# Projections with the tokens as weights: the sample's 32 tokens in full f32 through four column tiles

## The reference, cut to what matters

```python
# layer 0: v is the second half of the projection, then a layer norm over it
uv = jax.nn.gelu(x @ w_in)                 # x: (tokens, 1024), w_in: (1024, 4096)
u, v = uv[..., :D_A], uv[..., D_A:]        # D_A = 2048
# between the layers: keys and values of three branches
kv = (rmsnorm(h, kv_norm) @ kv_w)          # kv_w: (1024, 1536)
# layer 1: queries (and gates)
proj = xn @ w_in                           # the first 1024 columns are the queries
```

## Time and profile before

| | us |
|---|---|
| median of 3 runs (1818.1 to 1823.41) | 1822.81 |
| the profiled execution, its own time | 1806.65 |
| its span, first to last instruction | 1804.4 |

### The profile page before, as it was taken

One profiled execution on the slowest core, in us unless ns is written; L12 is line 12 of the kernel. 1 busy time (PEld: TensorE's weight loads), 2 busy tenths in 40 slices (PEclk: granted clock), 3 DMA queues, 4 the chain that ended last, 5 costly groups with the idle time before them and its releaser, 6 DMA issues.

```text
span 1804.4 us, 32338 instructions
## 1 busy us (share of the span) xinstructions
PE 1702.9 (94%) x13254; PEld 1583.0 (88%) x13254; DVE 804.7 (45%) x1326; ACT 537.7 (30%) x872; POOL 79.4 (4%) x134
## 2 busy tenths in 40 slices
PE   6999999999999999998999776999878999999998
PEld 6998899998999999997999544566568999999998
DVE  4325542344333333356164647986445333333333
ACT  4224211222222112133232434765342222212211
POOL 0000000000000000000000002543000000000000
PEclk8999888998999999998999987999998999999999
DMA  4292121222222222222232341000722222222221
GB/s 146 71 315 70 58 66 47 85 94 71 91 73 93 94 81 82 82 84 69 70 125 54 117 130 52 2 1 27 245 60 92 70 83 81 93 93 92 72 76 67
DMA packets 139296, 156.74 MB, mean 87 GB/s; under 512 B 11730, under 2 KB 127746, under 8 KB 138786
## 3 DMA queue, kind: packets, MB, share of 16 engines
q1 hardware_dynamic: 139122, 155.41, 27.0%
q10 hardware_dynamic: 80, 0.02, 0.0%
HBM read 149.58 MB, written 14.16 MB: 91 GB/s over the span
## 4 chain that ended last, share of the span: by engine, by line
PE 88%; DVE 4%; SPq 3%; issue 2%; ACT 2%; DMA 1%; DVEq 0%; ACTq 0%
PE PS L544 58%; PE PS L570 15%; PE PS L870 2%; PE PS L884 2%; PE PS L897 2%; SPq L486 2%; SPq L488 1%; PE PS L678 1%; PE PS L675 1%; PE PS L984 1%; PE PS L950 1%; PE PS L851 1%; PE PS L620 1%; ACT wh L1078 1%; PE PS L937 0%
## 5 line engine op out<-in xcount | busy, mean ns | idle before, releaser
L1401 DVE TENSOR_TENSOR wl<-raw,wh 128x2048 fp32r<-128x2048 f32 x106 | 242.7, 2290 | 410.5 <-ACT wh L1078 410.5
L544 PE MATMUL PS<-act0h,wh 128*128 128x272 f32 x1792 | 378.3, 293 | 10.7 <-DVE act0l L1874 5.9
L544 PE MATMUL PS<-act0l,wh 128*128 128x272 f32 x1792 | 376.0, 291 | 0.0
L544 PE MATMUL PS<-act0h,wl 128*128 128x272 f32 x1792 | 375.7, 291 | 0.0
L1078 ACT ACTIVATE wh<-raw 128x2048 fp32r<-128x2048 f32 x106 | 202.6, 1911 | 433.6 <-PE PS L544 432.2
L544 PEld LDWEIGHTS PS<-act0h,wh 128*128 128x128 f32 x1792 | 287.0, 192 | 11.6 <-DVE wl L1401 6.1
L544 PEld LDWEIGHTS PS<-act0l,wh 128*128 128x128 f32 x1792 | 286.4, 192 | 0.0
L544 PEld LDWEIGHTS PS<-act0h,wl 128*128 128x128 f32 x1792 | 285.8, 191 | 0.0
L570 PE MATMUL PS<-wh,act0h 128*128 128x256 f32 x560 | 161.0, 288 | 7.5 <-DVE act0l L1488 7.5
L570 PE MATMUL PS<-wl,act0h 128*128 128x256 f32 x560 | 159.4, 285 | 0.0
L570 PE MATMUL PS<-wh,act0l 128*128 128x256 f32 x560 | 159.3, 284 | 0.0
(11 more groups left out here) (270 smaller groups left out, 2327.7 us busy)
## 6 DMA issues: line engine op xcount, KB each, us to landing
raw<-in_ffn_w_gate SPq DMA_DIRECT2D x44, 512.0 KB
raw<-in_ffn_w_up SPq DMA_DIRECT2D x44, 512.0 KB
raw<-in_a_w_in SPq DMA_DIRECT2D x32, 512.0 KB
raw<-in_ffn_w_down SPq DMA_DIRECT2D x32, 512.0 KB
raw<-in_a_w_out SPq DMA_DIRECT2D x16, 512.0 KB
crows<-in_cache_kv_cmp SPq DMA_DIRECT2D x64, 128.0 KB, 2.1
cache<-in_cache_kv_slc SPq DMA_DIRECT2D x32, 256.0 KB, 5.0
cache<-in_state_kv_win SPq DMA_DIRECT2D x8, 1024.0 KB, 7.8
```

The source lines that it names most:

```text
L544: mm = pe.matmul(PS[:, 4 * ps + 2 * mt + h, 0:HALF], W[:, rs, k, mt * P:mt * P + P], Xp[:, k * T + h * HALF:k * T + h * HALF + HALF], star ...
L1401: dve.tensor_tensor(wl[:, rs, :, :], raw[:, rs, :, :], wh[:, rs, :, :].bitcast(F32), ALU.subtract).then_inc(w_ready, 1)
```

## The change

In the eighteen token-weight blocks the fifth token tile goes. In its place the 32 sample tokens are the stationary operand of 8 full f32 matmuls (no split: `few` holds the normed f32 activations, `raw` the f32 weights), each in one of four column tiles of 32: feature tile k goes to PSUM partitions 32 (k % 4) onward of bank 4*ps + 2, feature tiles 4 to 7 being added to 0 to 3. ScalarE copies the resulting 128 x 256 partial sums to SBUF (`part`), and one more full f32 matmul with a 128 x 32 selector (`sel`, a one where partition mod 32 is the column) adds the four groups into bank 4*ps + 3, from which ScalarE takes the sample's outputs.

- TensorE: the partials run first in an ordinary block, the gather (with a wait for ScalarE's copy, `f_st`) after the third of four token tiles. In the two fresh blocks the first loop takes tiles 0 and 2, then come the partials, tile 1, the gather and tile 3. `halves` is raised by two at the end of the block, no longer after the fourth tile.
- ScalarE: a copy of the partials before the outputs of the same block in v and kv; in q before the squares of the keys (q0), and after the split that follows the block before (q1 to q3).
- SyncE: a load of a v, kv or q block also waits until the partials of the block two before are done (`f_mm`), since they read `raw`; so does the first load of the mixing stage, for all of v's partials.
- GpSimd gathers the 32 tokens of the normed activations into `few` (three copies); VectorE builds the selector at the start in three additions.

```diff
+    f_ready, f_mm, f_st, f_sel = sem("few_tokens_ready"), sem("few_partials"), sem("few_partials_stored"), sem("few_selector")
@@ sync
+        def segment_few(at, w, c0, f0, m0, m1):
+
+            for m in range(m0, m1):
+                if m >= 2 or f0:
+                    sp.wait_ge(f_mm, f0 + m - 1)
+                load_item(m % 2, at[0] + m, *block_of(w, 0, KT, c0 + m * CW))
+
-        segment(at_v, a_w_in[0], 4, c0=DA)
+        segment_few(at_v, a_w_in[0], DA, 0, 0, 8)
...
+        sp.wait_ge(f_mm, 8)
         for c in range(2):
             segment(at_mix[c], a_w_in[0], 2, c0=c * D)
...
-        segment(at_kv, kv_w, 3)
-        segment(at_q, b_w_in[0], 2)
+        segment_few(at_kv, kv_w, 0, 8, 0, 6)
+        segment_few(at_q, b_w_in[0], 0, 14, 0, 4)
...
         sp.wait_ge(w_ready, at_wo[0] + 2)
+        sp.wait_ge(f_mm, 18)
@@ tensor, item_b
+            def partials():
+                for k in range(KT):
+                    c = 32 * (k % 4)
+                    mm = pe.matmul(PS[c:c + 32, 4 * ps + 2, 0:CW], few[:, k, :], raw[:, rs, k, :],
+                                   start=(k < 4), stop=(k >= 4))
+                mm.then_inc(f_mm, 1)
+
+            def gather():
+                pe.wait_ge(f_st, n - at_ + f0 + 1)
+                pe.matmul(PS[0:TD, 4 * ps + 3, 0:CW], sel[:, :], part[:, rs, :], start=True, stop=True)
...
             if fresh is None:
-                for t in range(TT):
-                    if t in (0, QT):
-                        pe.wait_ge(free[ps], 2 * use + (t == QT) + 1)
+                partials()
+                pe.wait_ge(free[ps], 2 * use + 1)
+                for t in range(QT):
                     for k in range(KT):
                         mm = products(t, k)
-                    if t in (QT - 1, QT):
-                        mm.then_inc(halves, 1)
+                    if t == QT - 2:
+                        pe.wait_ge(free[ps], 2 * use + 2)
+                        gather()
             else:
...
-                    for t in range(0, TT, 2):
+                    for t in range(0, QT, 2):
                         products(t, k)
-                for t in range(1, TT, 2):
+                pe.wait_ge(f_ready, 1 if f0 == 0 else 2)
+                partials()
+                for t in range(1, QT, 2):
                     for k in range(KT):
                         mm = products(t, k)
-                mm.then_inc(halves, 2)
+                    if t == 1:
+                        gather()
+            mm.then_inc(halves, 2)
...
@@ scalar
+        def partials(part, s, f):
+
+            act.wait_ge(f_mm, f + 1)
+            act.activation(part[:, s, :], PS[:, 4 * s + 2, 0:CW], ACT.Copy).then_inc(f_st, 1)
...
             def evac(i, s, unit, use):
                 c = bass.ds((2 * i + s) * CW, CW)
+                partials(part, s, f0 + 2 * i + s)
                 act.wait_ge(halves, 2 * unit + 1)
...
-                act.activation(dst[:, QT, c], PS[:, 4 * s + 2, 0:CW], func).then_inc(free[s], 1)
+                act.activation(dst[:, QT, c], PS[:, 4 * s + 3, 0:CW], func).then_inc(free[s], 1)
...
+        segment(at_kv, 3, rows_evac(kvtok, ACT.Copy, part_b, 8))
+        partials(part_b, 0, 14)
...
                 split(s, at_q[0] + q + 2, at_q[0] // 2 + 1, at_q[1] + q)
+            if q + 1 < NG:
+                partials(part_b, 1 - s, 15 + q)
@@ gpsimd
+        def few_tokens(j, few, n0):
+            pool.wait_ge(xs_ready, NORM_AT[j] + n0 + KT)
+            pool.tensor_copy(few[:, :, :], xs[:, n0:n0 + KT, TP:T]).then_inc(f_ready, 1)
+
+        few_tokens(0, few_v, 0)
+        few_tokens(2, few_k, 0)
+        few_tokens(2, few_q, KT)
```

More of the change, by code:

```diff
@@ L191, in build_program @@
     late = at("late", A_X, [P, C_LATE])
+    sel = at("sel", A_X + 6400, [P, TD])
     hgain = at("hgain", A_X + C_LATE * 4, [P, 3, HD])
@@ L197, in build_program @@
     xtok = at("xtok", A_P1, [P, TT, D])
+    few_v = at("few_v", A_P1, [P, KT, TD])
+    part_v = at("part_v", A_P1 + 1024, [P, 2, CW])
+    few_k, few_q = (at(f"few_{n}", A_V + 34816 + 1024 * j, [P, KT, TD]) for j, n in enumerate("kq"))
+    part_b = at("part_b", A_V + 36864, [P, 2, CW])
     gtok = at("gtok", A_P1 + 20480, [40, P])
@@ L563, in item_b @@
         def item_b(rs, ps, n, use, X, kn=KT, fresh=None):
-            xh, xl = X
+            (xh, xl), few, part, f0, at_ = X
             def products(t, k):
@@ L646, in _ @@
         norm(0)
-        segment(item_b, at_v, 4, act0, fresh=0)
+        pe.wait_ge(f_sel, 3)
+        segment(item_b, at_v, 4, (act0, few_v, part_v, 0, at_v[0]), fresh=0)
         slots_free(at_mix[0][2])
@@ L702, in _ @@
         norm(2)
-        segment(item_b, at_kv, 3, act0, fresh=2 * KT)
+        segment(item_b, at_kv, 3, (act0, few_k, part_b, 8, at_kv[0]), fresh=2 * KT)
         pe.wait_ge(xn_ready, 4 * KT)
-        segment(item_b, at_q, 2, act1)
+        pe.wait_ge(f_ready, 3)
+        segment(item_b, at_q, 2, (act1, few_q, part_b, 14, at_q[0]))
         slots_free(at_wo[2])
@@ L1092, in segment, with rows_evac @@
                 body(turns - 1, False)
-        def rows_evac(dst, func):
+        def partials(part, s, f):
+            act.wait_ge(f_mm, f + 1)
+            act.activation(part[:, s, :], PS[:, 4 * s + 2, 0:CW], ACT.Copy).then_inc(f_st, 1)
+        def rows_evac(dst, func, part, f0):
             def evac(i, s, unit, use):
                 c = bass.ds((2 * i + s) * CW, CW)
+                partials(part, s, f0 + 2 * i + s)
                 act.wait_ge(halves, 2 * unit + 1)
@@ L1113, in query_evac @@
             act.activation(q[:, QT, bass.ds(i, 1), :, s, :].rearrange("p x r d -> p (x r) d"),
-                           PS[:, 4 * s + 2, 0:CW].rearrange("p (r d) -> p r d", r=R), ACT.Copy).then_inc(free[s], 1)
+                           PS[:, 4 * s + 3, 0:CW].rearrange("p (r d) -> p r d", r=R), ACT.Copy).then_inc(free[s], 1)
         def none(i, s, unit, use):
@@ L1168, in _ @@
         split(1, 1, 0)
-        segment(at_v, 4, rows_evac(vt, ACT.Gelu_apprx_tanh))
+        segment(at_v, 4, rows_evac(vt, ACT.Gelu_apprx_tanh, part_v, 0))
         act.wait_ge(v_var, 1)
@@ L1211, in _ @@
         norm(2)
-        segment(at_kv, 3, rows_evac(kvtok, ACT.Copy))
+        segment(at_kv, 3, rows_evac(kvtok, ACT.Copy, part_b, 8))
+        partials(part_b, 0, 14)
         act.wait_ge(xn_ready, 4 * KT)
@@ L1511, in _ @@
         link(dve.memset(act0[1][:, KT * T:].bitcast(F32), 0.0))
+        dve.wait_ge(s_cst, 16)
+        dve.tensor_tensor(sel[:, :], ident[:, 0:TD], ident[:, TD:2 * TD], ALU.add).then_inc(f_sel, 1)
+        for j in range(2, 4):
+            dve.wait_ge(f_sel, j - 1)
+            dve.tensor_tensor(sel[:, :], sel[:, :], ident[:, TD * j:TD * j + TD], ALU.add).then_inc(f_sel, 1)
         for n in range(0, 2 * TT, 2):
```

## The result

| | us |
|---|---|
| kernel before, median of 22 runs (1809.09 to 1825.11) | 1820.34 |
| changed kernel, median of 22 runs (1814.25 to 1837.88) | 1828.19 |
| ratio changed / before, 95% interval | 1.0042 (1.0025 to 1.0058) |
| profiled execution of the changed kernel: its time, its span | 1833.87, 1832.1 |

The change costs 7.6 us by the ratio (4.6 to 10.6), where the forecast was 1.0 us faster. The time itself, 1828.19, lies in the wide range of 1812 to 1835 and 0.2 us above the case's own of 1816 to 1828. That it came so near is in part luck: the median of the kernel before moved down by 2.5 us, from 1822.81 in 3 runs to 1820.34 in 22.

What follows compares the result with a forecast made beforehand. TensorE was taken to bound the kernel, with 88% of the chain. Terms of -0.9 (v), -0.9 (kv) and +2.8 us (q) summed to 1.0 us faster, 1821.8 us; own range 1816 to 1828, wide range 1812 to 1835.

Steps and rivals of the forecast that it cites:

- the case's own: Whole kernel: the forecast's own range, 1816 to 1828 us, given chance 0.60, around 1821.8.
- the sum of the ordinary block: Each ordinary v, kv or q block: sample's tile out, partials and gather in, 14.26 to 13.06 us, saving 1.20.
- the clock behind v7's wait: TensorE after the idle stretch before v7's gather: 3 us at half rate, 1.5 us lost.
- The three waits: TensorE idle before three gathers: 7.7 us at v7 (DMA queue), 5.1 at kv0 (norm), 2.0 at q1 (gate weights).
- the pairwise rival: Partials: only two column tiles run at once, 1.88 us per block, kernel at 1834 us; chance 0.16.
- the one-after-another rival: Partials: no column tiles overlap, 2.65 us more in each of 14 blocks, kernel at 1859 us; chance 0.05.
- The 0.9 us of the outputs: End of v7: both output copies now follow the last matmul, putting 0.9 us more on the path.
- kv0: right: First kv block: gather waits 5.1 us behind the queries' norm, 1.9 lost to the clock; block loses 6.9 us.
- q: right: Four query blocks: 4 x 1.20 saved less 2.0 us idle at q1's gather, 2.8 us saved.
- kv and q in all: Six kv and four q blocks: kv 0.9 us slower in all, q 2.8 us faster.
- The wait at v7 doesn't come: Rival at v7: block 8's load overtakes the copies or they run quicker, v keeps 9 us, 1812.7; chance 0.14.
- Makes TensorE wait in each block: Rival in ordinary blocks: the gather order stops TensorE every time, some 1830 to 1860 us; chance 0.05.

Runs made afterwards that it cites:

- experiments 1 to 4: Changed kernel with window-state copies spread; kv0's partials copied mid-norm; gate weights loaded before q3; all three edits: ratios 0.9976, 0.9981, 1.0019, 0.9927 to the kernel before.
- all three waits gone (4): Changed kernel with copies spread, kv0's partials copied mid-norm, gate weights before q3, and block 8's load waiting only for v6's partials: 1809.17 us, ratio 0.9927.
- gather one block later (8): Changed kernel with copies spread, block 8's shorter wait, gate weights first, each gather behind the next block's partials; kv0's mid-norm copy left out: 1801.45 us, ratio 0.9895.
- experiment 7: The kernel before, unchanged, run for a second profiled execution: 1821.39 us, ratio 0.9997.
- experiments 9 to 12: Two more traces of either kernel, unchanged: 1813.66 and 1820.93 us for the kernel before, 1818.89 and 1821.62 us for the changed one.
- experiment 1: Changed kernel with the eight window-state copies moved from before block 8's load to behind the eight mixing loads, one each: 1815.09 us, ratio 0.9976.

## Why the prediction was wrong

The step that failed is the sum of the ordinary block, "14.26 - 2.85 + 1.05 + 0.60 = 13.06 us": it has no term for TensorE's coming back from the narrow tiles to the full array, 0.2 us twice per block, and the block takes 13.34 us. Over the blocks that count this is 4 of the 6 us by which the measured stages (5.0 us slower) miss the forecast (1.0 faster). The second step is the clock behind v7's wait, charged with 1.5 us and measured at 2.8. The three waits themselves, which the forecast worked out from the order of the queue and of ScalarE, were right in place and cause.

**The clock in all runs.** Each timed run has its span and its mean granted clock, and that carries the comparison past the few traces. The 27 runs of the kernel before are those beside experiments 1 to 4, the 22 of the changed one those of the result. Span x clock is what the span would be if all of it ran at 2.4 GHz, and the rest is what the clock took.

| kernel | runs | clock, median | span x clock, median | span x (1 - clock), median |
|---|---|---|---|---|
| before | 27 | 0.948 | 1723.7 | 94.6 |
| changed | 22 | 0.942 | 1720.5 | 105.9 |
| all three waits gone (4) | 5 | 0.945 | 1708.9 | 99.5 |
| gather one block later (8) | 5 | 0.947 | 1705.2 | 95.4 |

By these medians the changed kernel has 3.2 us less at full clock and 11.3 us more taken by the clock. The kernel before alone gave 1725.8 and 92.8 in the 11 runs of experiment 7, so 2 us in either column can't be told. In the traces the additional time at 1.2 GHz is 8.9 us in v (14.3 against 5.4 on the mean) and 7.0 in kv and q (12.0 against 5.0), and half of that, 8 us, is taken. The other 3 us, if they are more than scatter, lie elsewhere; the mixing stage is a candidate (experiments 9 to 12), and the traces at hand are too few to say. Not all that the clock took is lost: where TensorE idles anyway a lower clock costs nothing.

**The ordinary block: the term that was mis-sized.** Removed and added work stood at -2.85, +1.05 and +0.60. Partials took 1.00, as taken (four rounds at once; the pairwise rival and the one-after-another rival are out), and the gather 0.55. But the sum kept four token tiles at 4 x 2.85 = 11.40, and they take 11.80: 0.2 us each time the array comes back from the narrow tiles. For changes of shape the forecast charged 0.1 in the partials and 0.14 in the gather (0.60 against 0.46 alone), and the token tiles behind either stood at the price of tiles that follow each other. The saving is 0.93 and not 1.20, 0.28 us per block in some 14 blocks that count: 4 us. The forecast bounded such a cost by the L988 row at 0.2 us; that is what one return costs, and an ordinary block has two.

**v7: mechanism right, clock term too small.** The chain of causes held at each link: block 7's load behind v5's partials (96.60, said 94.8: v0's end 0.9 later, where 18 matmuls and not 12 still stood behind the last low part and two returns came in, and four blocks 0.28 longer), the queue in order (40.6 us, said 39.9), ScalarE before block 8's split, the copy behind it (139.03, said 136.6), 7.56 us idle (said 7.7). The clock is what failed here: 3 us at half rate were charged, and all of what followed, 6.4 us from 139.54 to 145.95, ran at 1.2 GHz, so 2.8 us were lost (gather 1.03 instead of 0.55, the 24 matmuls 5.39 instead of 3.05) and not 1.5. v7 ended at 145.95 instead of 141.8, of which 1.8 comes from the later issue, 0.7 from the queue, 1.3 from the clock and 0.2 from the return behind the gather. The 0.9 us of the outputs came as said. The forecast's own figures give v 1.1 us and not the 0.9 that it carried on: it took v7's end at 141.8 for that of before, 141.6.

**kv0: right.** Idle 4.70 (said 5.1), then a gather of 1.06 us and 24 matmuls in 4.55, where 0.55 and 3.05 are the price at full clock: 2.0 lost, said 1.9. The granted clock was 0.63 on the mean from 859.2 to 863.8 us. The block took 24.0 us (839.8 to 863.8), said 23.8; without its wait and the clock it is 17.3, where it was 17.2 before.

**q: right.** Idle 2.63 in the first trace, 1.10 and 2.23 in the others, 2.0 on the mean, as said. The clock stayed at 2.4 GHz behind it (mean 1.00 from 956.2 to 960 us).

**kv and q in all** were to save 1.9 us and cost 1.2 to 1.35. Of the difference of some 3.2 nine ordinary blocks x 0.28 are 2.5; the rest is q1's 0.6 in the first trace, and isn't told apart in the others.

**The sum.** With measured terms: 16 ordinary blocks x 0.93 = 14.9 and v0's 0.4 (16.7 us from 25.48 to 42.17, 17.1 before) saved, 15.3 in all, and nothing in kv0 beside its wait. Lost in the first trace: v7 7.6 + 2.8, kv0 4.7 + 2.0, q1 2.6, outputs 0.9, in all 20.6: 5.3 slower. With the mean waits of the three traces (7.2, 4.7, 2.0) and the same terms beside them it is 4.3. The stages of the traces give 2.9 + 0.9 + 1.2 = 5.0. The ratio gives 7.6, and its interval, 4.6 to 10.6, takes in 5.0; whether the other 2.6 us are real, and where they lie, isn't shown. The forecast netted a large saving against losses as large, and 1 us was what it left: an error of a tenth in either turned the sign. It named these pieces as unsure ("0.2 us more or less per block", "the clock 2 us"), and they fell nearly all to one side.

**The rivals.** "The wait at v7 doesn't come" is out as an account of the change; made to come true (experiment 1) the kernel took 1815.09, where 1812.7 was worked out; 14 blocks x 0.28 would more than close the gap. "Makes TensorE wait in each block" is out: only the three gathers named waited.

## What to carry to other kernels

A new reader of a buffer is a new condition on the next load into it, and with it on all that the queue holds behind: before adding one, move long transfers that nobody waits for (here eight copies of 1 MB) out from between the loads (here worth 10 us). A step that goes through another engine and back should be asked for a block later than it is made; that removed the waits but for 0.87 us at kv0, and a third of a microsecond per block. And where in a forecast a gain and its costs each are ten times their difference, the sign isn't known. What comes after a long stall is priced at the lower clock until the trace shows otherwise: here it was low behind stalls of 7.56 and 4.70 us and not behind one of 2.63.

## What the runs showed of the hardware

Four column tiles of 32 in full f32 run side by side: 16 records in 1.00 us, that is four rounds of 0.25 us at most, where one untiled record of 256 columns was worked out at 0.23. It holds whether neighbours in program order go to four tiles or two in a row to one (1.02).

Coming back from narrow tiles to 128 x 128 costs 0.2 us each time: 96 matmuls take 11.60 us behind one return and 11.80 behind two, and 96 x 0.1188 is 11.40.

The clock differs between executions of the same kernel at the same place: in the kernel before 3.4 to 35.7 us at 1.2 GHz in an attention stage of 149 to 159 us, in the changed one 37.5 to 61.6 in a mixing stage of 261 to 271 in which TensorE hardly idles. In the mixing stage time at half clock explains nearly all of the spread: 10.6 us of length for 24.1 us at 1.2 GHz, of which half would be 12. In the attention 32 us more at 1.2 GHz lengthen the stage by only 10. What sets either off was not tried.
